# A block of attention, mixed heads and routed experts on one core: every second expert row of two stretches is scaled and summed by GpSimd

## The chip, the cores and the metric

One core of a Trainium2 chip runs the whole program. The metric is the device time of one execution in microseconds (us). Engines are named as in the profile: PE is TensorE, DVE is VectorE, ACT is ScalarE, POOL is GpSimd, SP is SyncE.

## The reference, cut to what matters

All data is float32: 512 tokens of width 1024 pass a first block (attention with 16 heads, a gated convolution, a dense feed-forward) and a second block (stick-breaking attention, mLSTM heads, then PEER experts). The change lies in the last line of the second block:

```python
x = x + gate2 * peer(h2, w_q_peer, sub_keys, expert_u, expert_v)
# peer, per block of 128 tokens: 8 heads x 16 best experts = 128 slots per token
u = jnp.take(expert_u, ib, axis=0)
act = gelu(einsum('td,tkd->tk', xb, u))
vv = jnp.take(expert_v, ib, axis=0)
y = einsum('tk,tkd->td', gb * act, vv)
```

## The kernel before, in words

The tokens are worked in two halves of 256. Each half passes the weight blocks of 1 MB in a fixed order (`SEQ`): Q1, K1, V1, CG, XC, BG, then attention with the products GC, CP, GA filled in, AP, WO, UP (16), DN (16), QKM, Q2, K2, V2, the stick-breaking heads with VM and OM filled in, the mLSTM heads, WO2, PQ. SP loads the blocks into a ring of four.

The experts work on tiles of 128 tokens, 4 tiles with 128 slots each, `NS` = 512 slots. A slot is one row pair per token: an indirect DMA from POOL's queue gathers, for 128 tokens, 1024 values of u and 1024 of v (1 MB together) into one buffer `UV[r]`. Slots go in groups: two slots each up to slot 255, then four each. The experts of the first half (tiles 0 and 1, slots 0 to 255) run beside the second half's dense work. The list `TICKS` says after which weight blocks one step of the expert work is taken; some further steps lie within attention (`MORE`) and the stick-breaking heads. After the last weight block 198 slots are through; the rest runs alone. This part is called the tail. Up to slot 207 there are 6 buffers (`NUV0`), after it 16 (`NUV1`), in space that the dense work has left.

A step g of the generator `expert_steps` does this on DVE (lines 1404 to 1425): `coefficients(g - 1)` multiplies gate and gelu output; `accumulate(g - 1)` adds coefficient times v to `acc` for each slot of the group (line 1383, the first of a tile a plain scaling, line 1380); `dot_products(g)` forms u times token for the next group (line 1356); every eighth group the routing of the next 16 slots follows. ACT takes the gelu of the dots (line 961). From slot 198 on (`FIRST_PE`) every even slot's v goes through PE with a diagonal matrix of coefficients (line 534).

POOL walks the list `ENTRIES` in order (lines 493 to 515). For each entry it waits until the slot that held the buffer before is used up (`consumed`, which for a DVE slot waits on `acc_done`), then issues the indirect DMA (line 506). After each tile a negative entry brings the tile's x rows back from HBM (line 512), and `finish` (lines 1387 to 1398) adds PE's sum, multiplies by `gate2` and adds to x; POOL stores the result. `gate2` is an SBUF tensor of 128x1024 that ACT writes once at the end of the first half; it is read only by `finish`.

The work is ordered by hand in each engine's program; there is no scheduler. DVE's steps sit between the operations that the dense work waits for, such as the bias and maximum of attention scores (line 1476).

```python
                if BEFORE[e] is not None:
                    consumed(gp, BEFORE[e])
```

Of the kernel before, what the change touches and what calls it, by code (L numbers as in the profile page):

```python
# [5 lines left out]
F32 = mybir.dt.float32  # L6
# [115 lines left out]
    return s >= FIRST_PE and s % 2 == 0  # L122


PE_NO = [0]
for _s in range(NS):
    PE_NO.append(PE_NO[-1] + on_pe(_s))
END_GROUP = [GROUP_OF[NSLOT * t + NSLOT - 1] for t in range(4)]
FINISH_AT = {END_GROUP[t] + 2: t for t in range(3)}
ENTRIES = []  # L130
# [42 lines left out]
def build(nc, a, out):  # L173
    ctx = ExitStack()
    with ctx:
# [55 lines left out]
        acts = sb("acts", [P, 16])  # L231
        coef = sb("coef", [P, 16])
        cand = onehot[:, 0:256]

        PS = ctx.enter_context(nc.psum_tensor("PS", [P, 8, 512], F32))
        PSF = PS[:, :, :].rearrange("p b n -> p (b n)")
        kv_dram = nc.dram_tensor("kv_half", [P, 16 * T], F32, kind="Internal").ap()
        rel_neg = nc.dram_tensor("rel_neg", [NH1, 640], F32, kind="Internal").ap()
        x_dram = nc.dram_tensor("x_tokens", [S, D], F32, kind="Internal").ap()


# [63 lines left out]
        def col(name, k=0):  # L305
# [33 lines left out]
            "cand_done", "best_done", "gate_arg", "gate_exp", "gate_inv", "gated", "picked", "routed"))  # L339
        dot_done, gelu_done, coef_done, diag_done, moe_mm, acc_done, fin_a, fin_b, stored = (sem(n) for n in (  # L340
            "dot_done", "gelu_done", "coef_done", "diag_done", "moe_mm", "acc_done", "fin_a", "fin_b", "stored"))
        uv_in = [sem(f"uv_in{r}") for r in range(NUV1)]

        def tile_wait(eng, n, t):
# [23 lines left out]
        def consumed(eng, e):  # L368

            if e < 0:  # L370
                eng.wait_ge(stored, 16 * -e)
            elif on_pe(e):
                eng.wait_ge(moe_mm, PE_NO[e] + 1)
            else:
                eng.wait_ge(acc_done, e + 1 - PE_NO[e])

        block = ctx.enter_context(nc.Block())

# [2 lines left out]
        def _(sp):  # L381
# [31 lines left out]
            for n in range(NB):  # L413
                hf, kind, i = SEQ[n]
                if (hf, kind, i) == (0, V1, 0):
                    sp.wait_ge(rel_turned, 1)
                    sp.dma_start(rel_neg, REL).then_inc(rel_stored, 16)
                if (hf, kind, i) == (0, CG, 0):
                    sp.wait_ge(rel_stored, 16)
                if (hf, kind, i) == (0, XC, 0):  # L420
                    sp.dma_start(w_if[:, :, :], a["w_if"].rearrange("p (k g) -> p k g", g=2 * NML)).then_inc(w_if_loaded, 16)
                if (kind, i) == (CG, 0):
                    toeplitz(hf, 0)
                    toeplitz(hf, 1)
                    next_head = 2
                if (kind, i) == (WO, 0):
                    assert next_head == NH1
                if kind in FILL1 or kind == AP_:

                    f = n - NO[hf, FILL1[0], 0]  # L430
                    while next_head < NH1 and (TT * next_head - 5) * PER_ITEM <= (f - 3) * 2 * KT:
                        toeplitz(hf, next_head)
                        next_head += 1
                if (hf, kind, i) == (1, UP, 4):
                    sp.wait_ge(kv_stored, 16)
                    sp.wait_ge(pv_mm, 2 * NH1)
                    sp.dma_start(flat(40, 16 * T), kv_dram).then_inc(kv_loaded, 16)
                if (hf, kind, i) == (1, XC, 0):
                    spill_x(0)
                if (hf, kind, i) == (0, PQ, 0):  # L440
                    sp.wait_ge(silu_qk, 8)
                    for t in range(2):
                        evac_wait(sp, NO[0, VM, 1], t)
                    sp.wait_ge(hn_done, 24)
                    sp.dma_start(kv_dram, flat(20, 16 * T)).then_inc(kv_stored, 16)
                if (kind, i) == (PQ, 0):
                    sp.wait_ge(mixed_gain, 4 * (hf + 1))
                    sp.dma_start(SUBT, a["sub_t"].rearrange("c (m n) -> c m n", n=NK)).then_inc(sub_loaded, 16)
                    if hf == 0:
                        sp.dma_start(X[1], a["x_t"][1].rearrange("p (k t) -> p k t", t=T)).then_inc(x_loaded, 16)  # L450
                weights(n)
# [5 lines left out]
        def _(gp):  # L457
# [31 lines left out]
            def store(t):  # L489
                gp.wait_ge(fin_b, t + 1)  # L490
                gp.dma_start(out[0, t * P:(t + 1) * P, :], UV[BUF[-1 - t]][:, 0:D]).then_inc(stored, 16)

            store_after = {ENTRIES.index(-1 - t) + (13 if t else 3): t for t in range(3)}
            for p, e in enumerate(ENTRIES):
                r = BUF[e]
                if p == CHANGE:
                    gp.wait_ge(tok_copy, 18)
                    gp.wait_ge(tile_done, 2 * PE_BLOCK[NB])
                if p == CHANGE + NUV1 - 1:
                    gp.wait_ge(x_stored, 32)  # L500
                if BEFORE[e] is not None:
                    consumed(gp, BEFORE[e])
                if e >= 0:
                    if e % TOPK == 0:
                        gp.wait_ge(routed, e // TOPK + 1)
                    gp.indirect_dma_start(UV[r], None, a["expert_uv_2"],  # L506
                                          bass.IndirectOffsetOnAxis(ap=experts[:, e % 256:e % 256 + 1], axis=0))\
                        .then_inc(uv_in[r], 16)
                else:
                    t = -1 - e  # L510
                    gp.wait_ge(x_stored, 16 * (t // 2 + 1))
                    gp.dma_start(UV[r][:, 0:D], x_dram[t * P:(t + 1) * P, :]).then_inc(uv_in[r], 16)
                if p in store_after:
                    store(store_after[p])
            store(3)
# [770 lines left out]
        def _(dve):  # L1286
# [73 lines left out]
            def coefficients(g):  # L1360
# [2 lines left out]
                dve.wait_ge(gated, s0 // TOPK + 1)  # L1363
                if s0 >= 16:
                    dve.wait_ge(diag_done, PE_NO[s1 - 16])
                    dve.wait_ge(acc_done, s1 - 16 - PE_NO[s1 - 16])
                q, w = s0 % 16, s1 - s0
                dve.tensor_tensor(coef[:, q:q + w], acts[:, q:q + w], gates[:, s0 % 256:s0 % 256 + w], ALU.mult)\
                    .then_inc(coef_done, 1)
# [1 line left out]
            def accumulate(g):  # L1371
                dve.wait_ge(coef_done, g + 1)
                for s in range(*GROUPS[g]):
                    if not on_pe(s):
                        n = s - PE_NO[s]
                        v, c = UV[BUF[s]][:, D:2 * D], coef[:, s % 16:s % 16 + 1]
                        if s // NSLOT and n == (s // NSLOT) * NSLOT - PE_NO[s // NSLOT * NSLOT]:
                            dve.wait_ge(fin_b, s // NSLOT)
                        if n == (s // NSLOT) * NSLOT - PE_NO[s // NSLOT * NSLOT]:
                            dve.tensor_scalar(acc[:, :], v, c, None, ALU.mult).then_inc(acc_done, 1)  # L1380
                        else:
                            dve.wait_ge(acc_done, n)
# [2 lines left out]
            def finish(t):  # L1385
                s1 = NSLOT * (t + 1)
                x = UV[BUF[-1 - t]][:, 0:D]
                dve.wait_ge(moe_mm, PE_NO[s1])
                dve.wait_ge(acc_done, s1 - PE_NO[s1])
                shared = PE_NO[s1] > PE_NO[s1 - NSLOT]  # L1390
                if shared:
                    dve.tensor_tensor(acc[:, :], PS[:, 6:8, :].rearrange("p b n -> p (b n)"), acc[:, :], ALU.add)\
                        .then_inc(fin_a, 1)
                    dve.wait_ge(fin_a, 2 * t + 1)
                dve.tensor_tensor(acc[:, :], acc[:, :], gate2[:, :], ALU.mult).then_inc(fin_a, 1 if shared else 2)
                dve.wait_ge(fin_a, 2 * t + 2)
                dve.wait_ge(uv_in[BUF[-1 - t]], 16 * TIMES[-1 - t])
                dve.tensor_tensor(x, x, acc[:, :], ALU.add).then_inc(fin_b, 1)
# [517 lines left out]
```

## Time and profile before

| what | value |
|---|---|
| median of 3 runs | 2744.39 us (2738.85 to 2749.54) |
| the profiled execution's own time | 2737.65 us |
| its span, first to last instruction | 2735.9 us |
| mean granted PE clock | 0.897 |
| busy share: PE, DVE, ACT, POOL | 81%, 65%, 23%, 29% |
| HBM read, written | 790.27 MB, 6.33 MB |

The span is what the trace views divide up; some 2 us lie around it. Busy shares are means over stretches with different limits, so the views by stretch tell more. A row of the list in order of time gives start, duration, engine, line, operation and tiles, and in brackets how long the engine was idle before it and what released it.

### The profile page before, as it was taken

To read this page: it belongs to the slowest core of one execution; us is meant where nothing else is said; L and a number is where in the kernel's file an instruction comes from. 1 tells how busy PE (TensorE), PEld (TensorE's weight loads), DVE (VectorE), ACT (ScalarE), POOL (GpSimd) and SP (SyncE) were. 2 spreads that over 40 slices of the span, in tenths; PEclk is the share of its full clock that TensorE was granted. 3 is DMA by queue.
4 is the path that set the end of the run, shared out by engine and by line. 5 is a ranking of instruction groups with operands and counts; after the bars stand their busy time and mean duration, and the time that the engine had idled before them with its cause. 6 is when DMAs were issued, how large, how long until landed. Compare 5 with 4: busy or idle time off the path is not lost. (4 is left out here: it accounts for less than half of the span.)

```text
span 2735.9 us, 26218 instructions
## 1 busy us (share of the span) xinstructions
PE 2204.6 (81%) x9032; PEld 1638.1 (60%) x9032; DVE 1781.8 (65%) x3677; ACT 633.5 (23%) x1442; POOL 787.0 (29%) x544
## 2 busy tenths in 40 slices
PE   8999999999989999898999998888554555555545
PEld 6787788888768778677788776767111212212211
DVE  4761110003337778677777686767899999999985
ACT  2104212002322420562221126513111111111110
POOL 0000000000000244234433232224654655545651
PEclk9999999999989999999999998989777777777776
DMA  6874334443234699798999883548899999999996
GB/s 249 294 263 142 129 112 150 153 154 123 77 123 190 247 370 407 262 321 351 383 421 416 347 352 145 196 182 329 359 421 409 422 421 421 421 389 421 422 421 255
DMA packets 114724, 798.33 MB, mean 292 GB/s; under 512 B 13312, under 2 KB 16512, under 8 KB 19104
## 3 DMA queue, kind: packets, MB, share of 16 engines
q0 software_dynamic: 74880, 541.10, 48.8%
q1 hardware_dynamic: 39712, 255.56, 25.3%
q8 instruction: 72, 1.18, 0.2%
q14 instruction: 60, 0.49, 0.0%
HBM read 790.27 MB, written 6.33 MB: 291 GB/s over the span
## 5 line engine op out<-in xcount | busy, mean ns | idle before, releaser
L556 PE MATMUL PS<-reg,ring 128*128 128x256 f32 x6016 | 1348.6, 383 | 48.6 <-DVE reg L1453 10.8
L556 PEld LDWEIGHTS PS<-reg,ring 128*128 128x128 f32 x6016 | 1141.6, 192 | 226.7 <-issue 44.0
L506 POOL DMA_INDIRECT uv<-in_expert_uv,experts x322 | 518.8, 1611 | 1751.9 <-DVE experts L1338 862.7
L534 PE MATMUL PS<-uv,spare 128*128 128x512 f32 x248 | 184.2, 899 | 217.7 <-ACT spare L954 212.3
L1383 DVE SCALAR_TENSOR_TENSOR acc<-uv,coef,acc 128x1024 f32<-128x1024 f32 x256 | 328.9, 1285 | 9.1
L1356 DVE CUSTOM_DVE_ANT_0 uv<-uv,h_tok 128x1024 f32<-128x1024 f32 x226 | 269.0, 1220 | 49.1 <-DMA uv<-in_expert_uv,experts 48.7
L534 PEld LDWEIGHTS PS<-uv,spare 128*128 128x128 f32 x248 | 68.6, 294 | 331.0 <-issue 331.0
L534 PE MATMUL PS<-reg,spare 128*128 128x512 f32 x228 | 157.4, 843 | 116.9 <-ACT spare L954 110.9
L961 ACT ACTIVATE acts<-dots 128x2 f32<-128x2 f32 (+1 forms) x192 | 39.1, 204 | 776.1 <-DVE dots L1356 720.0
L534 PEld LDWEIGHTS PS<-reg,spare 128*128 128x128 f32 x228 | 57.9, 269 | 212.6 <-issue 212.6
L506 POOL DMA_INDIRECT reg<-in_expert_uv,experts x114 | 147.6, 1295 | 86.6 <-PE PS L534 58.3
L1640 DVE TENSOR_TENSOR reg<-PS,reg 128x256 f32<-128x256 f32 x16 | 6.5, 423 | 220.6 <-PE PS L556 220.6
L1356 DVE CUSTOM_DVE_ANT_0 uv<-uv,reg 128x1024 f32<-128x1024 f32 x96 | 115.1, 1222 | 31.8 <-DMA uv<-in_expert_uv,experts 31.8
L534 PE MATMUL PS<-ring,spare 128*128 128x512 f32 x152 | 92.0, 748 | 51.9 <-ACT spare L954 51.9
L506 POOL DMA_INDIRECT ring<-in_expert_uv,experts x76 | 111.3, 1465 | 35.8 <-issue 20.4
L553 PE MATMUL PS<-ring,reg 128*128 128x256 f32 x512 | 116.9, 383 | 0.0
L1356 DVE CUSTOM_DVE_ANT_0 reg<-reg 128x1024 f32<-128x1024 f32 x96 | 112.5, 1220 | 3.0 <-DMA reg<-in_expert_uv,experts 3.0
L553 PEld LDWEIGHTS PS<-ring,reg 128*128 128x128 f32 x512 | 96.1, 191 | 17.1 <-issue 4.9
L961 ACT ACT_TABLE_LOAD x59 | 75.7, 1283 | 112.8 <-issue 69.1
L534 PEld LDWEIGHTS PS<-ring,spare 128*128 128x128 f32 x152 | 34.6, 240 | 110.2 <-issue 110.2
L1534 DVE SCALAR_TENSOR_TENSOR uv<-ring,silu_c,uv 128x256 f32<-128x256 f32 x168 | 81.5, 485 | 6.0
L1476 DVE CUSTOM_DVE_ANT_0 reg<-PS,toep 128x128 f32<-128x128 f32 (+1 forms) x64 | 31.1, 485 | 82.1 <-PE PS L634 79.1
(248 smaller groups left out, 2194.3 us busy)
## 6 DMA issues: line engine op xcount, KB each, us to landing
ring<-in_weights SPq DMA_DIRECT2D x228, 1024.0 KB
uv<-in_expert_uv,experts POOLq DMA_INDIRECT x322
reg<-in_x_t SPq DMA_DIRECT2D x2, 1024.0 KB, 6.2
kv_half<-reg SPq DMA_DIRECT2D x1, 2048.0 KB, 12.2
reg<-in_sub_t SPq DMA_DIRECT2D x2, 1024.0 KB, 4.8
toep<-rel_neg SPq DMA_DIRECT2D x16, 128.0 KB
x_tokens<-reg SPq DMA_DIRECT2D x2, 1024.0 KB, 10.3
reg<-kv_half SPq DMA_DIRECT2D x1, 2048.0 KB
```

Source lines behind the costliest of these rows:

```text
L506: gp.indirect_dma_start(UV[r], None, a["expert_uv_2"], bass.IndirectOffsetOnAxis(ap=experts[:, e % 256:e % 256 + 1], axis=0))\
L534: mm = pe.matmul(PS[:, 6 + j, :], diag[:, n % 4, :], UV[BUF[s]][:, D + 512 * j:D + 512 * j + 512], start=begins, stop=ends, **LAX)
L553: mm = pe.matmul(out_tile(n, t), mv[:, t * P:(t + 1) * P], w, start=first and k == 0, stop=last and k == KT - 1)
L556: mm = pe.matmul(out_tile(n, t), w[:, t * P:(t + 1) * P], mv, start=first and k == 0, stop=last and k == KT - 1)
L961: act.activation(acts[:, s0 % 16:s0 % 16 + s1 - s0], dots[:, s0 % 16:s0 % 16 + s1 - s0], ACT.Gelu)\
L1356: dve.tensor_tensor_reduce(out=u, in0=u, in1=H2[s // 256][:, s // NSLOT % 2, :], scale=1.0, scalar=0.0, op0=ALU.mult, op1=ALU.add, accum_o ...
L1383: dve.scalar_tensor_tensor(acc[:, :], v, c, acc[:, :], ALU.mult, ALU.add).then_inc(acc_done, 1)
L1476: dve.tensor_tensor_reduce(out=PROB[:, i % 4, 0:w], in0=PS[:, i % 3, 0:w], in1=toep[:, hd % 2, w - 1::-1], scale=1.0, scalar=-NEG, op0=ALU ...
L1534: dve.scalar_tensor_tensor(ac, ring[:, n % NRING, k, :], silu_c[:, k:k + 1], ac, ALU.mult, ALU.add)\
L1640: dve.tensor_tensor(x[:, k, :], out_tile(n, t), x[:, k, :], ALU.add).then_inc(evac_sem(n, t), 1)
```

## The change

GpSimd takes over the odd slots 45 to 87 (22 slots, beside attention, AP and WO of the second half) and 145 to 197 (27 slots, from QKM to PQ). It does so when it comes to refill the slot's buffer: a scaling in place of v, a wait for it, an add onto `acc_pool`, a wait for that, then the refill. The first slot of each range is scaled straight into `acc_pool`. `acc_pool` lies in the space of `gate2`, whose rows are therefore stored to HBM at block Q1 3 of the second half, and loaded again for each tile behind its x rows, into the other half of the same buffer. `finish` of tiles 0 and 1 has one more add.

```diff
+def on_pool(s):
+    return s % 2 == 1 and (44 <= s < 88 or 144 <= s < FIRST_PE)
...
+        acc_pool = gate2
...
             else:
-                eng.wait_ge(acc_done, e + 1 - PE_NO[e])
+                eng.wait_ge(acc_done, DVE_NO[e] + 1)
...
+                if (hf, kind, i) == (1, Q1, 3):
+                    sp.wait_ge(tok_copy, 10)
+                    sp.dma_start(gate2_dram, gate2[:, :]).then_inc(gate2_stored, 16)
...
+            def accumulate(s):
+
+                n, v, c = POOL_NO[s], UV[BUF[s]][:, D:2 * D], coef[:, s % 16:s % 16 + 1]
+                gp.wait_ge(coef_done, GROUP_OF[s] + 1)
+                if n == POOL_NO[s // NSLOT * NSLOT]:
+                    if n:
+                        gp.wait_ge(fin_pool, s // NSLOT)
+                    else:
+                        gp.wait_ge(gate2_stored, 16)
+                    gp.tensor_scalar(acc_pool[:, :], v, c, None, ALU.mult).then_inc(pool_done, 1)
+                else:
+                    gp.tensor_scalar(v, v, c, None, ALU.mult).then_inc(pool_scaled, 1)
+                    gp.wait_ge(pool_scaled, POOL_SCALED[s] + 1)
+                    gp.wait_ge(pool_done, n)
+                    gp.tensor_tensor(acc_pool[:, :], v, acc_pool[:, :], ALU.add).then_inc(pool_done, 1)
...
-                if BEFORE[e] is not None:
+                if BEFORE[e] is not None and on_pool(BEFORE[e]):
+                    accumulate(BEFORE[e])
+                    gp.wait_ge(pool_done, POOL_NO[BEFORE[e]] + 1)
+                elif BEFORE[e] is not None:
                     consumed(gp, BEFORE[e])
...
                     gp.dma_start(UV[r][:, 0:D], x_dram[t * P:(t + 1) * P, :]).then_inc(uv_in[r], 16)
+                    gp.wait_ge(gate2_stored, 16)
+                    gp.dma_start(UV[r][:, D:2 * D], gate2_dram).then_inc(gate_in, 16)
...
-                    dve.wait_ge(acc_done, s1 - 16 - PE_NO[s1 - 16])
+                    dve.wait_ge(acc_done, DVE_NO[s1 - 16])
+                    if POOL_NO[s1 - 16]:
+                        dve.wait_ge(pool_done, POOL_NO[s1 - 16])
...
-                    if not on_pe(s):
-                        n = s - PE_NO[s]
+                    if not on_pe(s) and not on_pool(s):
+                        n = DVE_NO[s]
...
+                if POOL_NO[s1] > POOL_NO[s1 - NSLOT]:
+                    dve.wait_ge(pool_done, POOL_NO[s1])
+                    dve.tensor_tensor(acc[:, :], acc_pool[:, :], acc[:, :], ALU.add).then_inc(fin_pool, 1)
+                    dve.wait_ge(fin_pool, t + 1)
...
-                dve.tensor_tensor(acc[:, :], acc[:, :], gate2[:, :], ALU.mult).then_inc(fin_a, 1 if shared else 2)
+                dve.wait_ge(gate_in, 16 * (t + 1))
+                dve.tensor_tensor(acc[:, :], acc[:, :], UV[BUF[-1 - t]][:, D:2 * D], ALU.mult)\
+                    .then_inc(fin_a, 1 if shared else 2)
```

## Rows read from the trace of the kernel before

**Rows 1.** The page's span in 40 slices: DVE busy, and GB/s moved.

```profile
DVE  4761110003337778677777686767899999999985
GB/s 249 294 263 142 129 112 150 153 154 123 77 123 190 247 370 407 262 321 351 383 421 416 347 352 145 196 182 329 359 421 409 422 421 421 421 389 421 422 421 255
```

**Rows 2.** Busy time of each engine by stretch; the first line names the columns.

```profile
core 0: us, PE busy (x) PEld busy (x) DVE busy (x) ACT busy (x) POOL busy (x), PEclk, DMA share, GB/s
922.00:1102.00 180.00, 165.53 (x770) 136.84 (x768) 141.14 (x243) 32.98 (x83) 76.13 (x42) 0.99 0.96 380
1102.00:1250.00 148.00, 132.72 (x714) 101.50 (x715) 105.53 (x241) 94.73 (x181) 49.88 (x27) 0.95 0.84 296
1250.00:1327.00 77.00, 67.19 (x312) 57.29 (x312) 59.25 (x107) 13.75 (x31) 32.13 (x18) 0.98 0.94 370
1327.00:1556.00 229.00, 224.82 (x1040) 197.24 (x1039) 167.53 (x269) 44.68 (x116) 91.50 (x58) 1.00 1.00 412
1556.00:1644.00 88.00, 81.21 (x384) 64.46 (x384) 74.72 (x144) 23.07 (x53) 27.82 (x16) 0.98 0.79 309
1644.00:1790.00 146.00, 122.46 (x563) 97.08 (x564) 102.94 (x162) 80.88 (x105) 29.90 (x16) 0.89 0.41 153
1790.00:1912.00 122.00, 106.23 (x496) 91.47 (x496) 82.09 (x146) 31.38 (x72) 43.60 (x24) 0.92 0.74 277
1983.00:2710.00 727.00, 385.07 (x568) 146.16 (x567) 666.90 (x1329) 115.24 (x289) 378.21 (x281) 0.74 1.00 416
```

**Rows 3.** PE in order of time, rows with idle time ahead: three of 22.

```profile
1129.03 0.63 PE L645 MATMUL PS<-ident,reg 128*128 128x128 f32 x4 [0.39 <-ACT spare L1078]
...
1677.99 1.22 PE L711 MATMUL PS<-scr,tri 128*128 128x256 f32 x2 [4.19 <-DVE scr L1744]
...
1824.44 6.61 PE L579 MATMUL PS<-scr,ones_d 128*128 128x256 f32 x16 [5.28 <-ACT scr L1005]
```

**Rows 4.** The tile acc, forms with min/median/max ns and first and last start.

```profile
L1383 DVE SCALAR_TENSOR_TENSOR acc<-uv,coef,acc x256: 1283/1285/1287, 922.1 to 2715.8; 128x1024 f32<-128x1024 f32 x128
...
L1395 DVE TENSOR_TENSOR acc<-acc,gate x4: 1224/1225/1226, 1493.9 to 2723.0; 128x1024 f32<-128x1024 f32 x4
```

**Rows 5.** POOL's element-wise operations at the start, mean ns last before the bar.

```profile
L481 POOL TENSOR_SCALAR_AFFINE_SELECT spread<-spread 128x512 f32<-128x512 f32 x1 | 0.7, 655 | 0.0
...
L475 POOL TENSOR_SCALAR_AFFINE_SELECT tri<-tri 128x128 f32<-128x128 f32 x1 | 0.3, 292 | 0.0
```

**Rows 6.** Order of time: POOL's issue beside a DVE dot, and one beside none.

```profile
1122.98 1.22 DVE L1356 CUSTOM_DVE_ANT_0 uv<-uv,h_tok 128x1024 f32<-128x1024 f32 x1
1123.04 1.98 POOL L506 DMA_INDIRECT uv<-in_expert_uv,experts  x1 [0.30 <-issue]
...
1484.61 0.94 POOL L506 DMA_INDIRECT uv<-in_expert_uv,experts  x1 [0.30 <-issue]
```

**Rows 7.** Order of time in K2: refills of two steps, a dot that waited for one.

```profile
1602.96 1.98 POOL L506 DMA_INDIRECT uv<-in_expert_uv,experts  x1 [0.30 <-issue]
...
1608.37 1.98 POOL L506 DMA_INDIRECT uv<-in_expert_uv,experts  x1 [0.30 <-issue]
...
1621.49 1.23 DVE L1356 CUSTOM_DVE_ANT_0 uv<-uv,h_tok 128x1024 f32<-128x1024 f32 x1 [1.64 <-DMA uv<-in_expert_uv,experts]
```

**Rows 8.** Where the tail begins: the refill after slot 197, and a dot's wait.

```profile
1910.86 1.98 POOL L506 DMA_INDIRECT uv<-in_expert_uv,experts  x1 [0.30 <-issue]
...
1925.05 1.23 DVE L1356 CUSTOM_DVE_ANT_0 uv<-uv,h_tok 128x1024 f32<-128x1024 f32 x1 [1.84 <-DMA uv<-in_expert_uv,experts]
```

**Rows 9.** Tail by 10 us, columns as in Rows 2, after tile 1's and 2's finish.

```profile
2100.00:2110.00 10.00, 4.67 (x9) 1.84 (x8) 9.79 (x21) 0.90 (x3) 3.77 (x3) 0.84 0.90 361
...
2430.00:2440.00 10.00, 6.27 (x8) 2.35 (x8) 8.69 (x20) 0.90 (x3) 6.37 (x6) 0.66 0.65 231
```

**Rows 10.** The end on DVE: the last dot, and the last tile's multiplication by gate2.

```profile
2712.75 1.23 DVE L1356 CUSTOM_DVE_ANT_0 uv<-uv,reg 128x1024 f32<-128x1024 f32 x1 [1.24 <-DMA uv<-in_expert_uv,experts]
...
2723.04 1.22 DVE L1395 TENSOR_TENSOR acc<-acc,gate 128x1024 f32<-128x1024 f32 x1
```

More of the change, by code:

```diff
@@ L122, in on_pe @@
     return s >= FIRST_PE and s % 2 == 0
-PE_NO = [0]
+def on_pool(s):
+    return s % 2 == 1 and (44 <= s < 88 or 144 <= s < FIRST_PE)
+PE_NO, POOL_NO, DVE_NO = [0], [0], [0]
 for _s in range(NS):
     PE_NO.append(PE_NO[-1] + on_pe(_s))
+    POOL_NO.append(POOL_NO[-1] + on_pool(_s))
+    DVE_NO.append(_s + 1 - PE_NO[-1] - POOL_NO[-1])
+POOL_SCALED, _n = {}, 0
+for _s in range(NS):
+    if on_pool(_s) and POOL_NO[_s] > POOL_NO[_s // NSLOT * NSLOT]:
+        POOL_SCALED[_s] = _n
+        _n += 1
 END_GROUP = [GROUP_OF[NSLOT * t + NSLOT - 1] for t in range(4)]
@@ L238, in build @@
         rel_neg = nc.dram_tensor("rel_neg", [NH1, 640], F32, kind="Internal").ap()
+        gate2_dram = nc.dram_tensor("gate2_rows", [P, D], F32, kind="Internal").ap()
         x_dram = nc.dram_tensor("x_tokens", [S, D], F32, kind="Internal").ap()
@@ L341, in build @@
             "dot_done", "gelu_done", "coef_done", "diag_done", "moe_mm", "acc_done", "fin_a", "fin_b", "stored"))
+        gate2_stored, gate_in, pool_done, fin_pool = (sem(n) for n in ("gate2_stored", "gate_in", "pool_done", "fin_pool"))
+        pool_scaled = sem("pool_scaled")
         uv_in = [sem(f"uv_in{r}") for r in range(NUV1)]
@@ L1373, in accumulate @@
                 for s in range(*GROUPS[g]):
-                    if not on_pe(s):
-                        n = s - PE_NO[s]
+                    if not on_pe(s) and not on_pool(s):
+                        n = DVE_NO[s]
                         v, c = UV[BUF[s]][:, D:2 * D], coef[:, s % 16:s % 16 + 1]
-                        if s // NSLOT and n == (s // NSLOT) * NSLOT - PE_NO[s // NSLOT * NSLOT]:
+                        if s // NSLOT and n == DVE_NO[s // NSLOT * NSLOT]:
                             dve.wait_ge(fin_b, s // NSLOT)
-                        if n == (s // NSLOT) * NSLOT - PE_NO[s // NSLOT * NSLOT]:
+                        if n == DVE_NO[s // NSLOT * NSLOT]:
                             dve.tensor_scalar(acc[:, :], v, c, None, ALU.mult).then_inc(acc_done, 1)
@@ L1388, in finish @@
                 dve.wait_ge(moe_mm, PE_NO[s1])
-                dve.wait_ge(acc_done, s1 - PE_NO[s1])
+                dve.wait_ge(acc_done, DVE_NO[s1])
+                if POOL_NO[s1] > POOL_NO[s1 - NSLOT]:
+                    dve.wait_ge(pool_done, POOL_NO[s1])
+                    dve.tensor_tensor(acc[:, :], acc_pool[:, :], acc[:, :], ALU.add).then_inc(fin_pool, 1)
+                    dve.wait_ge(fin_pool, t + 1)
                 shared = PE_NO[s1] > PE_NO[s1 - NSLOT]
```

## The prediction

> **What bounds the kernel now.** The slices of the page come first [rows 1]. DVE is at 6 to 8 tenths from slice 15 on and at 9 in the tail; the traffic stands at 421 GB/s in most slices from the 30th on, and near it in slices 20 and 21. The stretches say the same in more detail [rows 2]. From 1327 to 1556 us (UP and DN) PE is 98% busy and the DMA engines are full. From 1983 to 2710 us the DMA share is 1.00 and DVE is busy for 667 of 727 us: the tail takes as long as its rows take to come in, and DVE is not far behind. The two ranges of the change lie elsewhere, in the stretches 1102 to 1327 and 1556 to 1912. There the DMA share is 0.41 to 0.94, PE lacks 15.3, 9.8, 6.8, 23.5 and 15.8 us of being full, 71 us in all, and DVE is at 67 to 85%. So these stretches end by PE's work plus what PE waits. What a shorter DVE step is worth there is what those waits hold of it.
>
> I therefore read PE in order of time and kept the idle times with a DVE step just ahead, directly or through ACT, which stands in line behind DVE's maxima and dots [rows 3]. They are 22: 12 from 1126 to 1250 us with 14.9 us together, 4 from there to 1320 us with 6.8, and 6 from 1590 to 1830 us with 15.0. The first is 0.39, the last 5.28 us.
>
> **What is removed.** 49 accumulations at 1.285 us [rows 4] leave DVE, 63 us of its busy time. A step shrinks from about 5.2 us (two accumulations, two dots at 1.22 [rows 6], the coefficients) to 3.9. An idle time of PE can give back at most 1.285 us for one step, or all of itself if it is shorter. Capped in this way, with neighbouring ones behind the same step counted once, the 22 give 8.8 + 3.5 + 6.9 = 19.3 us. That is the ceiling of the direct gain. It could be a few us higher where DVE is behind by more than one step.
>
> **What POOL gets.** 49 scalings and 47 adds of 128x1024. The trace has only one-input operations of POOL: 655 ns at 512 columns, 292 at 128 [rows 5], so 0.95 ns a column, and 1.15 us at 1024. I take this for the scaling. The add has two inputs: 1.15 us if the second is free, 2.3 if it costs as much again. I take 2.3, as both come from the same memory, and keep both ends. With the waits a slot costs 3.5 to 3.8 us, in all about 170 us of POOL. By the Trainium skill (GPSIMD Engine Reference, Performance versus the Vector engine) an add of 2048 columns takes 4497 ns; half of it is an estimate of 2.25 us, and the sum would be the same.
>
> POOL now issues a pair of refills in about 3.7 us (49.88 us for 27) [rows 2]. With a slot's arithmetic it has 7.2 to 8 us of work a step. By the counts of its refills, steps are 11, 8.6, 11, 18 and 10 us apart in the five stretches. On the mean it fits everywhere. In bursts it doesn't: in K2 two steps' refills are 5.4 us apart [rows 7], and other steps too are less than 7.2 us apart. Of the 19.3 us, 7.0 stand behind such close steps and 12.3 behind wide ones.
>
> **Who blocks whom.** A refill is issued in 0.94 us when DVE is quiet and in 1.98 when it starts 0.06 us into a dot: it ends 0.82 us after that dot does [rows 6]. So POOL waits until DVE's instruction with two SBUF inputs is over. The dots keep their 1.22 us beside it. What happens when POOL reads for 1.15 or 2.3 us and a dot arrives, no row shows: DVE may be untouched (0), or held for what is left. After the step's dots POOL's scaling and add run from some 3.7 to 7.4 us behind the step's start, so with wide steps they meet only short DVE work, with close ones the next step's accumulation. I take 2 us off the wide steps' 12.3 and count the close steps' 7.0 at nothing: **10 us gained**. By the Trainium skill (SBUF — State Buffer, Who interferes with whom) the shared pair is held by one engine for a whole instruction and the other fully blocks. The refill row agrees for POOL as the one that waits; by that rule DVE would wait too. That is the second rival.
>
> **Late refills.** The odd slot's refill moves back by POOL's 3.5 us, in a burst by up to 8. A refill has two or three steps to land. In K2 and V2 dots wait already for rows, 1.64 us once [rows 7]; there DVE falls behind by perhaps 3 us more, most of it in time in which it waits anyway. I take 1 us on the path, 0 to 4.
>
> **Where the tail begins.** The refill behind slot 197 starts at 1910.86; it moves to about 1914.5. Its dot has to wait some 3.7 us, but the next dots wait for rows in any case, 1.84 us at 1925.05 [rows 8]. I take 2 us of 0 to 3.7. All that follows waits for DMA and inherits it.
>
> **The gate's rows.** One store and four loads of 0.52 MB, each 1.25 us at 421 GB/s. The store meets a DMA share of 0.96 and a PE at 92% [rows 2]; it stands in SP's queue ahead of the weights of Q1 3, its semaphore is long set, and the ring of four covers it: 0.6 us, half of it. Tile 0's load falls in DN, where both PE and DMA are full [rows 2]: 0.6 too. Those of tiles 1 and 2 lie in the full tail and push every later row: 2.5 us. Tile 3's comes after the last row; the last dot is at 2712.75 and the gate is wanted at 2723.04 [rows 10], so it is hidden by 10 us. The waits on `gate_in` end before `finish` for the same reason: x lands ahead of it on the same queue.
>
> **Finish.** Two more adds of 1.22 us [rows 4]. Tile 0's lies in DN beside a full PE: 0. Tile 1's puts off PE's restart, the store and the refill that waits for the store; there the traffic drops to 361 GB/s for 10 us, and to 231 after tile 2 [rows 9], so the queue runs dry at that point and a delay counts: 1.2 us.
>
> **The sum.** -10 +1 +2 +0.6 +0.6 +2.5 +1.2 = -2.1 us, rounded to -3 for the steps in which DVE is behind by more than one. The profiled execution would go from 2737.65 to 2734.6, and the median, which is 6.7 us above it, from 2744.4 to **2741.4**. This kernel's runs can tell about 0.5%, 13.7 us, from no change.
>
> **The rivals.**
> *DVE keeps its whole gain.* If POOL never holds DVE and the bursts pass, the 19.3 us come in full, and DVE's lag over several steps adds a few more of the 36.7. Against costs of some 5 us this is -15 to -20: 2727. For it: the dots at 1.22 us beside POOL's issues. Against: close steps, in which POOL has 7.2 us or more of work. Chance 0.27.
> *POOL holds DVE.* The place is the close steps of attention, AP, WO and Q2 to V2, and the routing's operations with two inputs elsewhere. If each of POOL's two operations stops a DVE operation for half its time, DVE loses 1.7 us a slot and saves 1.285. At about 2.5 us a slot the loss of 1.2 us x 49 = 60 us of DVE time, of which a third reached PE at most in the ceiling above (19.3 of 63), is +19, with the 8 us of costs +27: 2771 at worst; at 2 us a slot it is +11 +8, 2763. From 1.285 us of blocking a slot this decides. The same would come of POOL's operations taking twice what I take, since refills then are late in every step. Chance 0.17, about 2760.
> *Gain and loss cancel*, as forecast: 2741, own range 2731 to 2755. Chance 0.56. In it I count that the gain is real but the DMA-bound parts take it back.
> That the arithmetic doesn't move to POOL can't be; the diff leaves no other engine for it.
>
> **How the numbers follow.** Faster by over 0.5% means under 2730.7 and goes with the first rival, 0.27; slower means over 2758.1 and goes with the second, 0.17; the rest is 0.56. The range takes most of both: 2723 to 2758.
>
> **What would show it.** The 256 accumulations of the uv buffers [rows 4] down to 207; POOL scalings near 1.15 and adds near 2.3 us, in 49 and 47 instances, and the two first scalings. PE's idle time in 1102 to 1327 and 1556 to 1912 down from 71 us by about 10. POOL busy in these stretches up from 183 us by 170. DVE operations of more than 1.23 (dots) or 1.29 us (accumulations) would show that POOL holds DVE; dots that wait for rows in K2, V2 and at 1914 to 1925 would show late refills. The tail from its first wide refill to the last row should grow by 3 to 4 us with traffic still at 421 GB/s. I am wrong if POOL's add takes 4 us or more, if DVE's long operations stretch, or if the stretches shrink by 20 us.

## The result, and the profile after

The changed kernel takes 2772.07 us (median of 4 runs, 2770.59 to 2774.47) against 2746.66 us (median of 4, 2738.85 to 2749.54) before: a ratio of 1.0107, with an interval of 1.0087 to 1.0127. At that ratio it is 29 us slower. The forecast was 2741.4 and its range ended at 2758. The profiled execution took 2771.38 us at a mean granted clock of 0.892, and before 2737.65 at 0.897. Times below that I worked out from ratios use 2744 us for the kernel before.

The page of the changed kernel comes first: its span, DVE, POOL and traffic in 40 slices, then its costliest groups, with busy us and mean ns behind the bar.

```profile
span 2769.6 us, 26325 instructions
...
DVE  4761110013337779577677686766799999999986
...
POOL 0000000000000244488634265638753656546552
...
GB/s 245 291 260 137 130 109 152 153 149 134 66 119 206 250 374 408 249 325 323 348 421 418 355 300 178 213 167 259 352 421 416 417 421 421 422 388 421 421 422 304
...
L1395 DVE CUSTOM_DVE_ANT_0 uv<-uv,h_tok 128x1024 f32<-128x1024 f32 x226 | 298.6, 1348 | 59.7 <-DMA uv<-in_expert_uv,experts 59.4
...
L522 POOL TENSOR_SCALAR uv<-uv,coef 128x1024 f32<-128x1024 f32 x47 | 144.3, 3070 | 1.7
...
L525 POOL TENSOR_TENSOR gate<-uv,gate 128x1024 f32<-128x1024 f32 x47 | 120.3, 2560 | 3.9
```

A dot product has gone from 1.22 us [rows 6] to a mean of 1.35, a scaling on POOL takes 3.07 us and an add 2.56. The stretches, with the columns of [rows 2]:

```profile
1102.00:1250.00 148.00, 131.11 (x691) 101.72 (x691) 103.83 (x234) 91.08 (x173) 99.52 (x49) 0.93 0.81 288
1250.00:1327.00 77.00, 64.87 (x311) 55.37 (x312) 61.66 (x95) 14.21 (x31) 67.18 (x33) 0.98 0.88 326
1327.00:1556.00 229.00, 218.51 (x988) 190.90 (x987) 164.57 (x262) 44.64 (x115) 104.24 (x65) 0.97 0.98 403
1556.00:1644.00 88.00, 80.41 (x347) 66.47 (x346) 66.36 (x127) 21.48 (x55) 34.66 (x18) 0.94 0.74 283
1644.00:1790.00 146.00, 126.93 (x587) 98.24 (x585) 99.74 (x147) 79.51 (x100) 99.28 (x48) 0.91 0.63 231
1790.00:1912.00 122.00, 102.66 (x466) 85.43 (x465) 76.83 (x128) 27.46 (x63) 60.58 (x29) 0.89 0.53 191
1983.00:2710.00 727.00, 377.37 (x568) 140.54 (x568) 674.66 (x1362) 118.34 (x296) 403.36 (x297) 0.76 1.01 417
```

In the five stretches of the two ranges POOL is busy for 361 us where [rows 2] give 183. DVE is busy for 408 where they give 425: 16 us less, not the 63 that the 49 accumulations took. PE lacks 75 us of being full, not 71 (the work lies some 10 to 40 us later behind the same marks, so this is a rough comparison). The tail's traffic and DMA share are what they were. PE's granted clock is lower in four of the six stretches before the tail (0.97 where it was 1.00 in UP and DN); no run separates what that costs from the waits that go with it.

I set the two traces beside each other by the start of each group's coefficient operation. After minus before, in us:

```
group   0    24    36    39    42    45    57    72    78    84    90    96   102   120   165
      +7.8  +6.6  +8.1 +11.2 +15.1 +21.0 +20.0 +23.4 +28.2 +29.5 +30.3 +35.3 +38.1 +37.7 +40.1
```

Group 0 lies ahead of all that the change touches. It stood at -4 to +8 us in the executions of all these kernels, so a single trace carries that much uncertainty. From there: attention (to group 36) gives nothing, AP, WO and the first UP blocks lose 13 us, QKM to V2 6 us, PQ and the hand-over to the tail 8 us, and the tail 2; what lies between them makes up the rest.

How DVE loses what it was given shows in order of time. Two places of the second half's AP and WO (start, duration):

```profile
1281.45 2.35 POOL L525 TENSOR_TENSOR gate<-uv,gate 128x1024 f32<-128x1024 f32 x1
1281.46 2.62 DVE L1670 TENSOR_TENSOR reg<-reg,spare 128x256 f32<-128x256 f32 x1
...
1290.55 2.85 POOL L525 TENSOR_TENSOR gate<-uv,gate 128x1024 f32<-128x1024 f32 x1
1291.10 3.38 DVE L1395 CUSTOM_DVE_ANT_0 uv<-uv,h_tok 128x1024 f32<-128x1024 f32 x1
...
1298.90 29.58 PE L595 MATMUL PS<-reg,ring 128*128 128x256 f32 x128 [4.12 <-DVE reg L1670]
```

An operation of 0.42 us (the same line at 1298.42) takes 2.62 us when POOL's add starts beside it, and a dot that starts inside an add ends 1.1 us after it: nearly all of its own 1.22 us comes when the add is over. Behind that dot the same line (L1670) took 2.05 us at 1296.00, this time beside a scaling of POOL, and PE, which needs its second instance, waited 4.12 us. What an add holds are operations with both inputs in SBUF. One that reads PSUM as well starts inside an add and keeps its 1.09 us:

```profile
1675.48 2.35 POOL L525 TENSOR_TENSOR gate<-uv,gate 128x1024 f32<-128x1024 f32 x1
...
1676.21 1.09 DVE L1787 SCALAR_TENSOR_TENSOR reg<-PS,reg 128x896 f32<-128x896 f32 x1 [2.45 <-PE PS L740]
```

In the kernel "Earlier" below, one of the same size with both inputs in SBUF took 3.11 us beside an add. In many places POOL goes from one slot to the next without a pause:

```profile
1204.55 1.96 POOL L543 DMA_INDIRECT uv<-in_expert_uv,experts  x1 [0.27 <-POOL gate L525]
1206.81 1.89 POOL L543 DMA_INDIRECT uv<-in_expert_uv,experts  x1 [0.30 <-issue]
1208.74 2.86 POOL L522 TENSOR_SCALAR uv<-uv,coef 128x1024 f32<-128x1024 f32 x1
1211.69 2.37 POOL L525 TENSOR_TENSOR gate<-uv,gate 128x1024 f32<-128x1024 f32 x1
1214.33 1.95 POOL L543 DMA_INDIRECT uv<-in_expert_uv,experts  x1 [0.27 <-POOL gate L525]
```

A step costs it 9.8 us here. I add up what the single DVE operations from 1126 to 1975 us take beyond the median of the same form before (my own sum over the rows in order of time): before 0.4 us, after 68.0 us in 46 operations, 28.8 of them in 16 dots. Of the 68.0, 56.3 us lie beside an add and 10.6 beside a scaling. This sum is called the excess below; rows of DVE overlap by a little, so it is a measure of holding and not a time lost. It is 1.39 us for each of the 49 slots, where 1.285 were saved.

### The profile page after: what moved, and what is told of

It is laid out like the page before. It is cut to its first block, busy times and chain, and to the rows that moved or that the text cites. A ratio compares the mean times of both kernels' runs of the same rounds, so it can differ in the third digit from the quotient of the medians.

```text
span 2769.6 us, 26325 instructions
## 1 busy us (share of the span) xinstructions
PE 2223.9 (80%) x9032; PEld 1651.8 (60%) x9032; DVE 1788.9 (65%) x3630; ACT 633.3 (23%) x1442; POOL 1016.6 (37%) x644
## 4 chain that ended last, share of the span: by engine, by line
POOL 18%; DMA 17%; issue 13%; DVE 10%; PE 4%; ACT 1%; DVEq 0%; POOLq 0%; ACTq 0%
DMA uv<-in_expert_uv,experts 16%; POOL uv L543 7%; POOL uv L522 5%; POOL gate L525 4%; PE PS L573 2%; PE PS L595 2%; DVE uv L1395 2%; DMA out<-uv 1%; DVE acc L1424 1%; DVE reg L1395 1%; POOL reg L543 1%; DVE ring L1395 1%; DVE onehot L1369 0%; DVE onehot L1373 0%; DVE picks L1375 0%
## 5 line engine op out<-in xcount | busy, mean ns | idle before, releaser
L595 PE MATMUL PS<-reg,ring 128*128 128x256 f32 x6016 | 1364.5, 387 | 45.9 <-DVE reg L1500 10.8
L595 PEld LDWEIGHTS PS<-reg,ring 128*128 128x128 f32 x6016 | 1153.4, 194 | 228.7 <-issue 37.1
L543 POOL DMA_INDIRECT uv<-in_expert_uv,experts x322 | 472.1, 1466 | 1566.7 <-DVE experts L1377 870.6
L1395 DVE CUSTOM_DVE_ANT_0 uv<-uv,h_tok 128x1024 f32<-128x1024 f32 x226 | 298.6, 1348 | 59.7 <-DMA uv<-in_expert_uv,experts 59.4
L1424 DVE SCALAR_TENSOR_TENSOR acc<-uv,coef,acc 128x1024 f32<-128x1024 f32 x207 | 270.0, 1304 | 7.4
L573 PEld LDWEIGHTS PS<-uv,spare 128*128 128x128 f32 x248 | 66.5, 285 | 340.3 <-issue 340.3
L573 PEld LDWEIGHTS PS<-reg,spare 128*128 128x128 f32 x228 | 56.3, 261 | 213.2 <-issue 213.2
L522 POOL TENSOR_SCALAR uv<-uv,coef 128x1024 f32<-128x1024 f32 x47 | 144.3, 3070 | 1.7
L525 POOL TENSOR_TENSOR gate<-uv,gate 128x1024 f32<-128x1024 f32 x47 | 120.3, 2560 | 3.9
L573 PEld LDWEIGHTS PS<-ring,spare 128*128 128x128 f32 x152 | 34.8, 242 | 107.7 <-issue 107.7
```

The source lines that it names most:

```text
L522: gp.tensor_scalar(v, v, c, None, ALU.mult).then_inc(pool_scaled, 1)
L525: gp.tensor_tensor(acc_pool[:, :], v, acc_pool[:, :], ALU.add).then_inc(pool_done, 1)
L543: gp.indirect_dma_start(UV[r], None, a["expert_uv_2"], bass.IndirectOffsetOnAxis(ap=experts[:, e % 256:e % 256 + 1], axis=0))\
L573: mm = pe.matmul(PS[:, 6 + j, :], diag[:, n % 4, :], UV[BUF[s]][:, D + 512 * j:D + 512 * j + 512], start=begins, stop=ends, **LAX)
L595: mm = pe.matmul(out_tile(n, t), w[:, t * P:(t + 1) * P], mv, start=first and k == 0, stop=last and k == KT - 1)
L1395: dve.tensor_tensor_reduce(out=u, in0=u, in1=H2[s // 256][:, s // NSLOT % 2, :], scale=1.0, scalar=0.0, op0=ALU.mult, op1=ALU.add, accum_o ...
```

## The experiments

All ratios are to the kernel before on the same chip. The first four kernels split the change. The medians before were 2743.77, 2742.52 and 2744.4 us in the three groups.

**Only the gate's rows.** No slot goes to POOL; the store, the four loads and the other buffer stay.

```diff
-    return s % 2 == 1 and (44 <= s < 88 or 144 <= s < FIRST_PE)
+    return False
```

> Leaves POOL's arithmetic out and gives all slots back to DVE; only the gate's rows still go through HBM (one store, four loads of 0.52 MB). Theory H (POOL's operations hold DVE) and theory L (POOL's 9.3 us of work a step makes refills late) both expect 3 to 5 us over the kernel before, my terms of 0.6 + 0.6 + 2.5, about 2750. Theory G (the gate's rows are what costs) expects 2765 or more.

Measured: 2744.59 us, ratio 1.0004 [0.9990, 1.0017]. The five pieces of 0.52 MB cost 1 us, within -2.7 to +4.7, where 3 to 5 were expected.

**The relief alone.** The odd slots' rows are neither scaled nor summed by anyone (but for the first of each range); all the waits of POOL stay.

```diff
-                    gp.tensor_scalar(v, v, c, None, ALU.mult).then_inc(pool_scaled, 1)
-                    gp.wait_ge(pool_scaled, POOL_SCALED[s] + 1)
                     gp.wait_ge(pool_done, n)
-                    gp.tensor_tensor(acc_pool[:, :], v, acc_pool[:, :], ALU.add).then_inc(pool_done, 1)
+                    gp.memset(acc_pool[:, 0:1], 0.0).then_inc(pool_done, 1)
```

> The 49 slots stay off DVE, but POOL's scaling and add of 47 of them are left out (a one-column memset stands for them), so these rows are missing from the result. It shows what DVE's relief of 63 us is worth alone. Theories H and L: gain of 10 to 19 us against gate_only, so 2730 to 2740. Rival R (relief on DVE reaches nothing, since PE bounds these stretches): as gate_only, within 4 us.

Measured: 2714.24 us, ratio 0.9892 [0.9853, 0.9931]. That is 31 us below the gate's rows alone, give or take 11 by the two intervals, and more than the 10 to 19 expected. The excess is 1.5 us.

**POOL busy, but it only writes.** Five fillings of `acc_pool` with zeros take the place of the arithmetic; the rows are again left out.

```diff
+                    for i in range(4):
+                        gp.wait_ge(pool_done, n)
+                        gp.memset(acc_pool[:, :], 0.0).then_inc(pool_scaled, 1)
+                        gp.wait_ge(pool_scaled, 4 * POOL_SCALED[s] + i + 1)
+                    gp.memset(acc_pool[:, :], 0.0).then_inc(pool_done, 1)
```

> POOL's scaling and add of 47 slots are replaced by five memsets of 128x1024, about 5.2 us that only write (the 47 rows are missing from the result). POOL is as long busy as with the arithmetic, but reads nothing. Theory H: DVE's dots are back at 1.22 us, the time falls to that of drop within 4 us. Theory L: refills are as late as in the changed kernel, so the time stays at 2765 to 2775.

Measured: 2732.97 us, ratio 0.9958 [0.9942, 0.9974], 18 us above the relief alone (give or take 12). If holding were all, 4 at most were expected; if late refills were, 2765 to 2775. The groups of this kernel:

```profile
L1396 DVE CUSTOM_DVE_ANT_0 uv<-uv,h_tok 128x1024 f32<-128x1024 f32 x226 | 269.9, 1222 | 69.3 <-DMA uv<-in_expert_uv,experts 68.7
...
L524 POOL MEMSET gate<- 128x1024 f32 x188 | 179.7, 956 | 8.1
```

POOL is busy for 4.8 us a slot, the dots keep 1.222 us, and what grows is their wait for rows. From 1126 to 1975 us (in total, times, longest) it is

```profile
DVE uv L1396 <- DMA uv<-in_expert_uv,experts: 65.4, 32, 4.9
```

where the relief alone has 48.6. By the starts of the groups some 8 us are lost in groups 36 to 44 (AP and WO: from -6.4 to -1.5 us against the kernel before, where the relief alone goes from -10.3 to -13.5). There the steps are 8.7 us apart with the relief alone and 9.7 here. So the 18 us are in the main the cost of late refills. They aren't free of holding: the excess is 9.8 us, nearly all of it in short operations that start inside a filling and end with it (the same line takes 0.22 us elsewhere):

```profile
1142.05 0.95 POOL L524 MEMSET gate<- 128x1024 f32 x1
1142.12 0.91 DVE L1363 TENSOR_SCALAR soft_e<-best_v 128x16 f32<-128x16 f32 x1
```

Three such rows overlap at a time, so less than 9.8 us is lost by them.

**POOL's work without the relief.** DVE accumulates every slot as before, and POOL's two operations are done as well, with the same shapes, into `acc_pool`, which is then not used. Here POOL first waits for DVE's accumulation, and `finish` has a one-column operation in place of its new add.

```diff
-                    gp.tensor_scalar(v, v, c, None, ALU.mult).then_inc(pool_scaled, 1)
+                    gp.tensor_scalar(acc_pool[:, :], v, c, None, ALU.mult).then_inc(pool_scaled, 1)
...
-                    if not on_pe(s) and not on_pool(s):
+                    if not on_pe(s):
```

> POOL does its scaling and add on all 49 rows into a scratch, and DVE accumulates them all as well, so nothing is relieved; the result is right without POOL's sum. Against gate_only it shows the price of POOL's work alone. If price and relief add up, keep minus gate_only is changed minus drop. Theory H: 30 to 45 us over gate_only, 2780 to 2795, dots at 1.45 us or more in the two ranges. Theory L: about as much, but with dots at 1.22 us and long waits for rows.

Measured: 2810.8 us, ratio 1.025 [1.0215, 1.0286]. The work on POOL costs 67 us over the gate's rows (30 to 45 were expected), and the relief gives 31. With the 1 us of the gate's rows the sum is +38; the change shows +29, which the intervals allow. The price is also higher here than in the change, since the kept accumulations are held too: 13 of them take up to 3.47 us in place of 1.285.

The next four take POOL's operations and the two ranges apart.

**Scaling alone, add alone.** Each leaves the other operation out, so that the odd rows enter the sum not at all in the first and unscaled in the second.

```diff
-                    gp.tensor_tensor(acc_pool[:, :], v, acc_pool[:, :], ALU.add).then_inc(pool_done, 1)
+                    gp.memset(acc_pool[:, 0:1], 0.0).then_inc(pool_done, 1)
```

> POOL scales 47 rows in place (2.9 to 3.3 us each) but doesn't add them, so they are missing from the result. Drop stands at 0.989 of the kernel before, the changed kernel at 1.011. Theory H1 (what holds DVE is the time in which POOL reads, about 1.15 us of the scaling and 2.36 of the add): a third of the 40 us between write_only and changed comes back here, and POOL is less long busy than in write_only, so 2725 to 2738. Rival H2 (every POOL instruction holds DVE for its whole length): scaling is the longer of the two, so 2742 or more. In H1 a dot that meets it is at most 1.2 us longer, in H2 up to 3.

```diff
-                    gp.tensor_scalar(v, v, c, None, ALU.mult).then_inc(pool_scaled, 1)
-                    gp.wait_ge(pool_scaled, POOL_SCALED[s] + 1)
```

> POOL adds 47 unscaled rows (2.36 us each), the scaling is left out, so the sum is not weighted. It also bounds a version in which ACT scales. H1: two thirds of the hold remain, but POOL has only 7 us of work a step, so refills are hardly late: 2735 to 2750, dots up to 2.36 us longer. H2: less than half of the hold, 2728 to 2738, below scale_only.

Measured: scaling alone 2715.92 us, 0.9912 [0.9882, 0.9941]; add alone 2737.93 us, 0.9984 [0.9969, 0.9998]. The forms of POOL and of the dots, first of the kernel with scaling alone (min/median/max ns in the second row):

```profile
L522 POOL TENSOR_SCALAR uv<-uv,coef 128x1024 f32<-128x1024 f32 x47 | 148.3, 3156 | 1.4
...
L1395 DVE CUSTOM_DVE_ANT_0 uv<-uv,h_tok x226: 1152/1219/2517, 907.9 to 2017.5; 128x1024 f32<-128x1024 f32 x113
```

And of the kernel with the add alone:

```profile
L523 POOL TENSOR_TENSOR gate<-uv,gate 128x1024 f32<-128x1024 f32 x47 | 117.8, 2507 | 1.0
...
L1393 DVE CUSTOM_DVE_ANT_0 uv<-uv,h_tok x226: 1152/1219/3365, 911.2 to 2046.8; 128x1024 f32<-128x1024 f32 x113
```

The scaling takes longer than the add and costs only 5 us over the relief, less than either theory expected; its excess is 5.9 us. The add costs 25 us, with an excess of 48.0 us in 29 operations. Each of the two costs is good to some 12 us, their difference of 20 to 9. So in this arrangement it is the add that holds DVE most. Both together cost 59 us over the relief.

**One range alone.** 22 slots in the first, 27 in the second.

```diff
-    return s % 2 == 1 and (44 <= s < 88 or 144 <= s < FIRST_PE)
+    return s % 2 == 1 and 44 <= s < 88
```

> Only the slots 45 to 87 (attention, AP, WO) are on POOL; the result is complete. In the two traces the first range and what follows it up to the 48th group lost 13 us, the second 17. If the loss sits in the close steps of AP and WO: 2756 to 2762, more than half of it for 22 of 49 slots. If it goes by the number of slots: 2757. Either way the first range alone is slower than the kernel before by 8 us or more; under 2750 speaks against the hold as the cause there.

The other kernel has `144 <= s < FIRST_PE` instead, and one wait of `finish` fits its single use of `acc_pool`.

> Only the slots 145 to 197 (QKM to PQ) are on POOL; the result is complete. If the loss goes with the hold a slot, 27 slots give 14 to 18 us, 2758 to 2764, and first_range and second_range together give the changed kernel's 29 us. If the late refills where the tail begins decide, this one has nearly all of the loss, 2765 or more. If the wide steps around the stick-breaking heads pay, it is under 2750.

Measured: 2755.46 us, 1.0053 [1.0035, 1.0071], and 2762.55 us, 1.0067 [1.0041, 1.0093]: +15 and +18 us. No part of the change gains in one range what it loses in the other.

The last four ask whether another arrangement would help.

**Earlier.** POOL sums the odd slot ahead of the refill of the even slot of its group, not behind it, and so meets other operations of DVE.

```diff
+                if BEFORE[e] is not None and BEFORE[e] >= 0 and on_pool(BEFORE[e] + 1):
+                    accumulate(BEFORE[e] + 1)
                 if BEFORE[e] is not None and on_pool(BEFORE[e]):
-                    accumulate(BEFORE[e])
```

> Same slots and the same two POOL operations, with a complete result, but POOL does them as soon as the coefficients are there, ahead of the pair's two refills. The add then starts about 3 us behind the step's start in place of 6.6, near the end of its dots and not in the next step. Scaling alone costs 2 us and add alone 24 over drop, both together 58. Theory P (the scaling costs by pushing the add into the next step's DVE work and the dense evacuations): near the sum of the two, 2740 to 2752. Theory L (what costs is how late the refills get): the even refill gets later too, so 2770 or more.

Measured: 2771.6 us, 1.0102 [1.0078, 1.0126], with an excess of 68.2 us as before this edit, now in 68 operations. The sum is the same and its parts aren't: the scaling now stands beside the step's dots, and 32 us of the excess lie beside a scaling, 36 beside an add. POOL waits too, so that a scaling takes 3.9 us on the mean:

```profile
1133.29 4.99 POOL L522 TENSOR_SCALAR uv<-uv,coef 128x1024 f32<-128x1024 f32 x1 [1.44 <-DVE coef L1410]
...
1134.42 1.22 DVE L1396 CUSTOM_DVE_ANT_0 uv<-uv,h_tok 128x1024 f32<-128x1024 f32 x1
...
1135.57 2.05 DVE L1396 CUSTOM_DVE_ANT_0 uv<-uv,h_tok 128x1024 f32<-128x1024 f32 x1
...
1725.56 2.35 POOL L525 TENSOR_TENSOR gate<-uv,gate 128x1024 f32<-128x1024 f32 x1
1725.75 3.11 DVE L1792 SCALAR_TENSOR_TENSOR reg<-reg 128x896 f32<-128x896 f32 x1
```

The dots wait 66.5 us for rows, 13 more than in the change. So this order doesn't help, and the run doesn't separate holding from late refills (2740 to 2752 was expected if only the meeting of the add with the next step counted, 2770 or more with late refills).

**The add in four parts of 256 columns.**

```diff
-                    gp.tensor_tensor(acc_pool[:, :], v, acc_pool[:, :], ALU.add).then_inc(pool_done, 1)
+                    for j in range(4):
+                        part = slice(256 * j, 256 * j + 256)
+                        if j == 3:
+                            gp.wait_ge(pool_part, 3 * POOL_SCALED[s] + 3)
+                        gp.tensor_tensor(acc_pool[:, part], v[:, part], acc_pool[:, part], ALU.add)\
+                            .then_inc(pool_done if j == 3 else pool_part, 1)
```

> The add in four parts of 256 columns, else as the changed kernel, with a complete result. Theory H (a DVE operation that meets a POOL add waits for all of it, up to 2.36 us): now it waits for one part of some 0.65 us, so most of the 24 to 40 us of hold comes back, 2745 to 2758, longest dots under 2 us. If POOL takes the pair again at once for the next part: 2768 or more and dots of 3.4 us as before.

Measured: 2795.12 us, 1.0184 [1.0162, 1.0206]. Its add, in order of time, with the dots beside it:

```profile
1288.95 5.43 POOL L529 TENSOR_TENSOR gate<-uv,gate 128x256 f32<-128x256 f32 x4
1289.51 1.75 DVE L1400 CUSTOM_DVE_ANT_0 uv<-uv,h_tok 128x1024 f32<-128x1024 f32 x1
...
1291.19 1.74 DVE L1400 CUSTOM_DVE_ANT_0 uv<-uv,h_tok 128x1024 f32<-128x1024 f32 x1
```

And POOL's group for it, and the dots' wait for rows from 1126 to 1975 us:

```profile
L529 POOL TENSOR_TENSOR gate<-uv,gate 128x256 f32<-128x256 f32 x188 | 185.4, 1007 | 7.6
...
DVE uv L1400 <- DMA uv<-in_expert_uv,experts: 97.3, 36, 10.2
```

A held dot now loses 0.5 us at a time instead of up to 2.2, as expected, and the excess falls to 40.7 us; the time expected with it, 2745 to 2758, was far off. Four parts take 4.0 us against 2.56: a part takes 0.72 us at the least, so 2.9 of the 4.0 are the parts themselves and the rest is POOL waiting between them. POOL's step is longer, and the dots wait 97.3 us for rows, where the change has 53.5. The 27 us of holding that it saved are paid for by 44 us of waiting.

**Fewer slots.** Every fourth slot of both ranges (25 slots), and every second one of narrower ranges (24).

```diff
-    return s % 2 == 1 and (44 <= s < 88 or 144 <= s < FIRST_PE)
+    return s % 4 == 1 and (44 <= s < 88 or 144 <= s < FIRST_PE)
```

> Only every fourth slot of the same two ranges, 24 or so of 49, with a complete result. POOL then has room in every second step. Theory L or P (cost grows with how full POOL is): less than half of the loss, 2742 to 2750. A fixed price a slot: half of the loss, 2757.

```diff
-    return s % 2 == 1 and (44 <= s < 88 or 144 <= s < FIRST_PE)
+    return s % 2 == 1 and (44 <= s < 66 or 152 <= s < 178)
```

> Odd slots 45 to 65 and 153 to 177 only, 24 of 49, where steps are mostly 9 us or more apart (attention's first part; stick-breaking and mLSTM heads, WO2); the result is complete. If the loss is made in the close steps of AP, WO, Q2 to V2 and PQ, as I read the two traces: 2738 to 2748, at or under the kernel before. A fixed price a slot: 2757.

Measured: 2752.69 us, 1.0039 [1.0021, 1.0057], with an excess of 28.3 us, and 2747.84 us, 1.0018 [1.0002, 1.0033], with 23.3. The first lies between what was expected for a cost that grows with POOL's load (2742 to 2750) and for a fixed price a slot (2757), the second at the upper end of 2738 to 2748. Where both slots of a group stay on DVE, the list in order of time shows the two accumulations in one row; these two sums count them one by one. They are 1.13 and 0.97 us a slot, under the 1.285 saved, and still neither kernel beats the kernel before: what DVE gains is not the whole account. The kernels that did beat it don't compute the whole weighted sum.

## Why the prediction was wrong, point by point

The parts as the experiments give them, each from two ratios: the gate's rows +1; the relief -31 (relief alone against the gate's rows); POOL busy for 4.8 us a slot +18 (writing against the relief); POOL reading (one tensor in the scaling, two in the add), and some 0.9 us more of it a slot, +41 (the change against writing). The sum is +29. The first is good to some 4 us, the last to 7, the two in the middle to 11 or 12.

**What is removed: the ceiling was too low.** 19.3 us were given as the most that 63 us of DVE time can be worth; the relief alone gives 31. The text had said "a few us higher"; it was 12, give or take 11. Against the kernel before, the starts of the groups with the relief alone stand at -0.5 us at group 22 and -13.5 at 44, at -7.8 at 72 and -20.4 at 102. The first range so gives 13.0 where 8.8 + 3.5 were forecast, and the second, with the hand-over, 12.6 where 6.9 were. It was the second that fell short. There the forecast had kept 6 of PE's idle times with 15.0 us, while the trace before has 17 behind DVE or ACT, with 34.8 us, from 1590 to 1830. That the others gave the rest is likely and not shown.

**What POOL gets: the scaling was mis-sized, and this failed first.** 1.15 us were taken from the 0.95 ns a column of the affine selects [rows 5]; measured are 3.07 us, and never less than 2.86. Those selects read no coefficient for each partition, and the row was taken over to an operation of another kind without a wider bound. The add was right: 2.3 against 2.34 at the least and 2.56 on the mean. So a step takes POOL 9.8 us, not 7.2 to 8, and "on the mean it fits everywhere" was false where the steps were given as 8.6 us apart, and hardly true where they were 10. The second rival had said it near its end: the same would come of POOL's operations taking twice what I take. They took 5.6 us a slot against 3.45, 1.6 times as much.

**Who blocks whom: the step that carried the sum.** This is where the forecast failed. It took 2 us off the wide steps' gain for holding, counted the close steps' 7.0 us at nothing, and had no term by which a step could lose: -10 us in all. In its place stand -31 of relief and +41 of POOL reading. Measured is an excess of 68.0 us of DVE time in the change, 48.0 with the add alone. The second rival's mechanism is what happened, and its threshold was passed by a little: DVE loses 1.39 us a slot and saves 1.285. Its 2771 at worst fits the time by luck. By its own sum that figure wants 2.5 us a slot; with 1.39 it gives 5 us of DVE time, a third of it on the path, and with the 8 us of costs about +10, or 2754. Most of the rest is the late refills, 18 us where that sum has 1. Nor is the place only that of close steps: with 24 slots of wide steps the excess is 23.3 us. By the Trainium skill (SBUF — State Buffer, Who interferes with whom) the engine that holds the shared pair holds it for a whole instruction. For the add the trace agrees, 0.42 us becoming 2.62 and a dot 3.38. For the scaling it does so only in part: with the scaling alone a dot beside it took at most 2.52 us, 1.3 more than alone, and the excess is 5.9 us in 49 slots.

**Late refills: 1 us forecast, 18 measured** where POOL is busy for 4.8 us a slot and holds only short operations. With 3.2 us a slot (scaling alone) it is about 5, though these differences are good to some 12 us only. It looks as if the cost comes where POOL's step fills up the time between two steps, as in AP and WO; no run shows the point itself. This also accounts for the 59 us of both operations against 5 and 25: the add alone turned 48 us of excess into 25 us, at that rate 68 make 35, and with the 18 for late refills it is 53 of 59. This last is an estimate, not shown: no run has the full excess with an idle POOL, and the two kernels with fewer slots show that the excess alone doesn't set the time.

**Where the tail begins, the gate's rows, finish.** Without the adds in finish, 3.7 us were forecast for the gate's rows. The kernel with these alone shows 1, with an interval of -2.7 to +4.7: it doesn't tell the two apart, and the term is small either way. The tail grows by 2 us of the 3 to 4 said. The hand-over was too cheap: groups 90 to 102 lose 8 us, the 2 us were for one late refill, while POOL comes out of PQ behind by several:

```profile
1948.80 2.86 POOL L522 TENSOR_SCALAR uv<-uv,coef 128x1024 f32<-128x1024 f32 x1
1951.74 2.85 POOL L525 TENSOR_TENSOR gate<-uv,gate 128x1024 f32<-128x1024 f32 x1
1954.86 1.70 POOL L543 DMA_INDIRECT uv<-in_expert_uv,experts  x1 [0.27 <-POOL gate L525]
```

The refill that stood at 1910.86 [rows 8] and was to move by 3.7 us is issued at 1954.86. Of these 44 us, some 35 are the delay of all the work up to there.

**The signs named ahead.** The accumulations went from 256 to 207 as said. POOL's busy time in the five stretches rose by 178 us (170 said), though the second range now reaches past them, to 1954. PE's idle time didn't fall by 10. Dots stretched, which the text had named as the sign of holding. Of the conditions named for being wrong, that one came about; the add was near its size, and what was far off was the scaling, for which I had named no limit.

## What to carry to other kernels

Before arithmetic is handed to GpSimd, its time for the very form of instruction has to be measured, and set beside what is left between two of its DMA issues in the busiest stretch; here 5.6 us of arithmetic a slot used that up, and the refills went late. A GpSimd add of two SBUF operands took from VectorE up to what it lasts wherever an operation with two SBUF inputs started inside it: 1.39 us a slot were lost to save 1.285. Operations that read PSUM kept their time. Cutting the add into parts shortened each hold and lengthened the whole, and that was worse.

## What the runs showed of the hardware that was not expected

- POOL's multiplication of 128x1024 by a coefficient per partition takes 2.86 us at the least, more than its add of two tensors (2.34). It holds DVE's operations with two SBUF inputs only in its first part, while the add does so to its end: of 18 dots that started inside an add of the changed kernel 16 were held, the longest for 2.2 us. Where dots start behind a scaling that has had to wait itself ("Earlier"), they take 2.05 us. Short operations of one input it holds to its end: 0.98 us for one of 0.22 us, at 1308.09 in the changed kernel.
- POOL's fillings of 128x1024 (0.956 us) leave the dots at 1.222 us, and hold short operations of one input (0.17 to 0.22 us) to their end, up to 0.91 us.
- An add of 256 columns takes 0.72 us at the least and one of 1024 columns 2.34: per column a fifth more. The mean of 1.01 us in the kernel with four parts has POOL's waits in it.
- The first part of a scaling, as here: the coefficients, 0.15 us elsewhere, end 1.14 us after the scaling has begun, and the accumulation that follows beside the same scaling keeps its 1.28 us (changed kernel, order of time):

```profile
1326.53 1.57 DVE L1409 TENSOR_TENSOR coef<-acts,gates 128x2 f32<-128x2 f32 x1
1326.96 2.86 POOL L522 TENSOR_SCALAR uv<-uv,coef 128x1024 f32<-128x1024 f32 x1
...
1328.14 1.28 DVE L1424 SCALAR_TENSOR_TENSOR acc<-uv,coef,acc 128x1024 f32<-128x1024 f32 x1
```

Why an operation with two SBUF inputs that a scaling holds is through 1.1 to 1.4 us after its start, and one that an add holds only at its end or behind it, was not taken further.
